# Attention output items later among the units, two expert loads sent earlier, four idle products ahead of the gather

## What is computed

```python
for l in range(DEPTH_2):                      # DEPTH_2 = 1
    h = rms_norm_2(x, norm_mix_w[l])
    p = h @ w_in[l]
    y_rw = rwkv7_mixer(p[..., :RW_COLS], ...)  # 8 heads of 64, a recurrence over tokens
    y_fox = fox_mixer(p[..., RW_COLS:], ...)   # 8 heads of attention with forget gates
    x = x + concatenate([y_rw, y_fox]) @ w_out[l]
    h = rms_norm_2(x, norm_ffn_w[l])
    x = x + hierarchical_moe(h, ...)           # 64 experts, 2 for each token
# rwkv7 step: S = S * w_t + (S a_t) b_t^T + v_t k_t^T ;  y_t = S r_t
# an expert:  (silu(x @ w_gate) * (x @ w_up)) @ w_down,  1024 x 512, 1024 x 512, 512 x 1024
```

## Time and profile before

| | |
|---|---|
| median of 3 runs | 1488.3 us (1487.18 to 1490.58) |
| the profiled execution's own time | 1499.18 us |
| its span in the profile | 1497.3 us |
| TensorE busy | 1129.1 us, 75% |
| VectorE, ScalarE, GpSimd busy | 342.0, 218.3, 68.2 us |
| read from HBM | 461.41 MB |
| granted TensorE clock, mean | 0.891 of full |

### The profile page before, as it was taken

One profiled execution on the slowest core, in us unless ns is written; L12 is line 12 of the kernel. 1 busy time (PEld: TensorE's weight loads), 2 busy tenths in 40 slices (PEclk: granted clock), 3 DMA queues, 4 the chain that ended last, 5 costly groups with the idle time before them and its releaser, 6 DMA issues.

```text
span 1497.3 us, 35673 instructions
## 1 busy us (share of the span) xinstructions
PE 1129.1 (75%) x15922; PEld 816.4 (55%) x15922; DVE 342.0 (23%) x993; ACT 218.3 (15%) x598; POOL 68.2 (5%) x119
## 2 busy tenths in 40 slices
PE   7999999999999887976565665666565666666565
PEld 4886578654885855754444444444444444444443
DVE  2544226520573144111111111111111111111111
ACT  1162106310152201110000000000000000000000
POOL 1100010000110110000000000000000000000000
PEclk9989999999999689998898889788888889888988
DMA  8733234215110069999999999999999999999997
GB/s 285 272 96 116 87 113 169 86 57 185 57 57 4 3 254 375 427 427 429 428 429 428 429 428 429 429 428 429 428 428 429 429 429 429 428 427 429 429 428 315
DMA packets 69029, 463.41 MB, mean 309 GB/s; under 512 B 14789, under 2 KB 18278, under 8 KB 44390
## 3 DMA queue, kind: packets, MB, share of 16 engines
q1 hardware_dynamic: 64784, 459.76, 74.5%
q10 hardware_dynamic: 4182, 2.72, 0.7%
HBM read 461.41 MB, written 1.05 MB: 309 GB/s over the span
## 4 chain that ended last, share of the span: by engine, by line
DMA 53%; PE 8%; DVE 1%; issue 1%; ACT 0%; SPq 0%; POOLq 0%; DVEq 0%; POOL 0%
DMA weight_slots<-in_exp_w_down_dram 53%; PE bank L2332 4%; PE bank L2323 1%; PE bank L2315 1%; PE bank L2297 0%; PE bank L2349 0%; ACT work_region L2253 0%; SPq L2167 0%; DVE normed_features L2454 0%; PE bank L2303 0%; DVE tokens L2532 0%; POOLq L2207 0%; DVE normed_features L2431 0%; DVE tokens L2514 0%; DVE tokens L2517 0%
## 5 line engine op out<-in xcount | busy, mean ns | idle before, releaser
L2323 PE MATMUL bank<-weight_slots,work_region 128*32 128x128 f32 x5120 | 182.2, 303 | 123.0 <-DMA weight_slots<-in_exp_w_up_dram 100.6
L2323 PEld LDWEIGHTS bank<-weight_slots,work_region 128*32 128x32 f32 x5120 | 157.0, 122 | 150.0 <-DMA weight_slots<-in_exp_w_up_dram 110.7
L2332 PE MATMUL bank<-weight_slots,work_region 128*32 128x256 f32 x1376 | 115.7, 489 | 90.8 <-DMA weight_slots<-in_exp_w_down_dram 88.1
L2323 PE MATMUL bank<-work_region 128*32 128x128 f32 x2560 | 92.7, 306 | 61.7 <-DMA work_region<-in_exp_w_up_dram 52.4
L2332 PEld LDWEIGHTS bank<-weight_slots,work_region 128*32 128x32 f32 x1376 | 58.7, 134 | 134.4 <-issue 98.2
L2323 PEld LDWEIGHTS bank<-work_region 128*32 128x32 f32 x2560 | 79.5, 123 | 75.3 <-DMA work_region<-in_exp_w_up_dram 57.5
L2253 ACT COPY work_region<-bank 128x256 f32<-128x256 f32 x64 | 23.8, 372 | 603.6 <-PE bank L2332 603.6
L2489 DVE TENSOR_SCALAR work_region<-work_region 128x128 f32<-128x128 f32 x128 | 38.5, 343 | 285.3 <-PE bank L2340 285.3
L534 PE MATMUL bank<-weight_slots,normed_features 128*128 128x512 f32 (+2 forms) x288 | 101.1, 508 | 2.1 <-DVE normed_features L792 2.1
L2332 PE MATMUL bank<-work_region 128*32 128x256 f32 x672 | 55.8, 484 | 45.5 <-DMA work_region<-in_exp_w_down_dram 44.8
L2500 DVE TENSOR_TENSOR work_region<-work_region,bank 128x128 f32<-128x128 f32 x64 | 23.9, 373 | 281.9 <-PE bank L2323 281.9
(11 more groups left out here) (431 smaller groups left out, 1253.2 us busy)
## 6 DMA issues: line engine op xcount, KB each, us to landing
weight_slots<-in_exp_w_up_dram SPq DMA_DIRECT2D x43, 2048.0 KB, 41.0
weight_slots<-in_exp_w_down_dram SPq DMA_DIRECT2D x43, 2048.0 KB, 40.7
weight_slots<-in_exp_w_gate_dram SPq DMA_DIRECT2D x43, 2048.0 KB, 41.7
work_region<-in_exp_w_gate_dram SPq DMA_DIRECT2D x21, 2048.0 KB, 41.8
work_region<-in_exp_w_up_dram SPq DMA_DIRECT2D x21, 2048.0 KB, 40.9
work_region<-in_exp_w_down_dram SPq DMA_DIRECT2D x21, 2048.0 KB, 40.7
weight_slots<-in_w_in_dram SPq DMA_DIRECT2D x16, 2048.0 KB, 9.9
weight_slots<-in_w_out_dram SPq DMA_DIRECT2D x6, 2048.0 KB, 8.5
```

The costliest lines, as they stand in the source:

```text
L2323: mm = nc.tensor.matmul(B[bank][BLK * j:BLK * (j + 1), 0:P], x[:, c], w[u][:, c, j * P:(j + 1) * P], start=c == 0, stop=c == KC - 1, tile_ ...
L2332: mm = nc.tensor.matmul(B[7][BLK * j:BLK * (j + 1), 0:256], hidt[u][:, BLK * k:BLK * (k + 1)], w_down[u][:, k, j * 256:(j + 1) * 256], sta ...
```

## The change

Three things. (a) In ORDER, and alike in TensorE's and ScalarE's programs, FO0 goes behind P21, FO1 behind TK1, FO2 behind MV1, FO3 behind F51. (b) The units' buffers are laid out slot by slot, so that slot 4 holds nothing that is read after item WV1 and slot 1 nothing that is read after the chunks' products; SyncE sends down 0 into slot 4 after WV1 and up 0 into slot 1 after chunk_made 4. The other two of EARLY stay where they were. (c) TensorE makes four products of 128 by 512 into a bank that is overwritten next, between the ranks and the gather.

```diff
@@ -1077,28 +1077,25 @@
-    room45 = carve(slot[:, 4:6].rearrange("p s n -> p (s n)"))
-    qt, kt = room45(4, T), room45(4, T)
-    pt = room45(4, 4, P)
-    sqk = room45(MT * 2 * NH, HD)
+    room4, room5 = carve(slot[:, 4]), carve(slot[:, 5])
+    qt, kt = room4(4, T), room4(4, T)
+    sqk = room4(MT * 2 * NH, HD)
+    pt = room5(4, 4, P)
-    room45 = carve(slot[:, 4:6].rearrange("p s n -> p (s n)"))
-    am, wu = room45(MT, NH, P), room45(MT, 2, NH, HD)
-    rbt, rkt = room45(MT, NH, CHUNK), room45(MT, NH, CHUNK)
-    reads = room45(2, CT, T)
-    a_, rx = reads[:, 0], reads[:, 1]
-    inverse_t, spare = room45(MT, NH, CHUNK), room45(MT, NH, CHUNK)
-    room01 = carve(slot[:, 0:2].rearrange("p s n -> p (s n)"))
-    btok, ktok, vtok = room01(MT, RW), room01(MT, RW), room01(MT, RW)
-    wt = room01(MT, CT, P)
-    kx = room01(CT, T)
-    state = room01(NCH, CT, HD)
-    ei = room01(CT, T)
+    room4, room5 = carve(slot[:, 4]), carve(slot[:, 5])
+    am, wu = room4(MT, NH, P), room5(MT, 2, NH, HD)
+    a_, rx = room4(CT, T), room5(CT, T)
+    reads = slot[:, 4:6, MT * NH * P:MT * NH * P + CT * T].rearrange("p x (i t) -> p x i t", i=CT)
+    inverse_t, spare = room4(MT, NH, CHUNK), room4(MT, NH, CHUNK)
+    rbt, rkt = room5(MT, NH, CHUNK), room5(MT, NH, CHUNK)
+    room0, room1 = carve(slot[:, 0]), carve(slot[:, 1])
+    vtok, wt, state = room0(MT, RW), room0(MT, CT, P), room0(NCH, CT, HD)
+    btok, ktok, kx, ei = room1(MT, RW), room1(MT, RW), room1(CT, T), room1(CT, T)
-    room_state = carve(state.rearrange("p q i d -> p (q i d)")[:, KC * LORA_W - D:])
-    f8 = room_state(MT, P)
-    kk_inv, ct = room_state(T), room_state(T)
+    room_tiles = carve(slot[:, 5, SLOT - 2 * MT * NH * CHUNK:])
+    f8 = room_tiles(MT, P)
+    kk_inv, ct = room_tiles(T), room_tiles(T)
@@ -1132,8 +1129,8 @@
-    ORDER = """TA0 TA1 AR0 AR1 FO0 KR0 KR1 TV0 TV1 FO1 P20 P21 FO2 P40 P41 FO3 P80 P81 TK0 TK1 G40 G41 MV0 MV1 Q0 Q1 TB0 TB1 F50 F51
-        BONUS WU0 WV0 WU1 WV1 WT0 WT1""".split()
+    ORDER = """TA0 TA1 AR0 AR1 KR0 KR1 TV0 TV1 P20 P21 FO0 P40 P41 P80 P81 TK0 TK1 FO1 G40 G41 MV0 MV1 FO2 Q0 Q1 TB0 TB1 F50 F51
+        FO3 BONUS WU0 WV0 WU1 WV1 WT0 WT1""".split()
@@ -1169,9 +1166,13 @@
                 sp.wait_ge(S["rkv_done"], 2 * (h + 1))
                 dst = slot[:, WO2_S[h], :].rearrange("p (k n) -> p k n", k=KC)
                 sp.dma_start(dst, wout[0, :, h * 512:(h + 1) * 512].rearrange("(k p) n -> p k n", p=P)).then_inc(loaded[WO2_S[h]], 16)
+            sp.wait_ge(S["item_made"], ORDER.index("WV1") + 1)
+            load_first_experts(sp, a, mem, EARLY[0:1])
+            sp.wait_ge(S["chunk_made"], 4)
+            load_first_experts(sp, a, mem, EARLY[1:2])
             sp.wait_ge(S["bonus_ready"], MT)
             sp.wait_ge(S["y_made"], MT)
-            load_first_experts(sp, a, mem, EARLY)
+            load_first_experts(sp, a, mem, EARLY[2:])
             for i in range(2):
                 sp.wait_ge(S["out_done"], 3 + i)
                 load_first_experts(sp, a, mem, LATE[i:i + 1])
@@ -1342,26 +1343,26 @@
 
             take(am[:, 0, :, 0:HD], "TA0", NH, HD)
             take(am[:, 1, :, 0:HD], "TA1", NH, HD)
-            fox_out(0)
             whole(vtok[:, 0], "TV0")
             whole(vtok[:, 1], "TV1")
+            for m in range(MT):
+                take(P2[:, m], f"P2{m}", NH, CHUNK)
+            fox_out(0)
+            for m in range(MT):
+                nc.scalar.copy(P4[:, m], view(bank(f"P4{m}")[:, :], NH, 2, CHUNK)[:, :, 0]).then_inc(S["power_copied"], 1)
+            for m in range(MT):
+                nc.scalar.copy(P8[:, m], view(bank(f"P8{m}")[:, :], NH, 2, CHUNK)[:, :, 1]).then_inc(S["power_copied"], 1)
+            for m in range(MT):
+                whole(ktok[:, m], f"TK{m}")
             fox_out(1)
             for m in range(MT):
-                take(P2[:, m], f"P2{m}", NH, CHUNK)
+                take(am[:, m, :, HD:P], f"MV{m}", NH, HD)
             fox_out(2)
             for m in range(MT):
-                nc.scalar.copy(P4[:, m], view(bank(f"P4{m}")[:, :], NH, 2, CHUNK)[:, :, 0]).then_inc(S["power_copied"], 1)
+                take(Q[:, m], f"Q{m}", NH, CHUNK)
+            for m in range(MT):
+                whole(btok[:, m], f"TB{m}")
             fox_out(3)
-            for m in range(MT):
-                nc.scalar.copy(P8[:, m], view(bank(f"P8{m}")[:, :], NH, 2, CHUNK)[:, :, 1]).then_inc(S["power_copied"], 1)
-            for m in range(MT):
-                whole(ktok[:, m], f"TK{m}")
-            for m in range(MT):
-                take(am[:, m, :, HD:P], f"MV{m}", NH, HD)
-            for m in range(MT):
-                take(Q[:, m], f"Q{m}", NH, CHUNK)
-            for m in range(MT):
-                whole(btok[:, m], f"TB{m}")
             src = bank("BONUS")
             nc.scalar.copy(bonus.rearrange("p m h -> p (m h)"), src[:, 0:MT * NH]).then_inc(S["act_took"], 1)
             for m in range(MT):
@@ -1616,21 +1617,18 @@
             turn("TA1", a_, 1)
             pe.wait_ge(S["scaled"], 5)
             of_features("AR", aa)
-            fox_out(0)
             of_features("KR", kx)
             pe.wait_ge(S["shifted"], 14)
             turn("TV0", v_, 0)
             turn("TV1", v_, 1)
-            fox_out(1)
             for m in range(MT):
                 pe.wait_ge(S["n_turned"], m + 1)
                 of_blocks(f"P2{m}", NT[:, m], N[:, m])
-            fox_out(2)
+            fox_out(0)
             for m in range(MT):
                 pe.wait_ge(S["power_turned"], m + 1)
                 pe.wait_ge(S["g_ready"], 1)
                 of_two(f"P4{m}", P2T, m, slice(0, 2))
-            fox_out(3)
             for m in range(MT):
                 pe.wait_ge(S["power_turned"], MT + m + 1)
                 needs(f"P4{m}")
@@ -1638,6 +1636,7 @@
             pe.wait_ge(S["ends_ready"], 1)
             turn("TK0", ei, 0)
             turn("TK1", ei, 1)
+            fox_out(1)
             for m in range(MT):
                 pe.wait_ge(S["power_turned"], 2 * MT + m + 1)
                 needs(f"P8{m}")
@@ -1645,6 +1644,7 @@
             for m in range(MT):
                 needs("KR0", "KR1", f"TV{m}")
                 of_blocks(f"MV{m}", AKT[:, m], view(vtok[:, m], NH, HD), HD)
+            fox_out(2)
             for m in range(MT):
                 pe.wait_ge(S["no_turned"], m + 1)
                 pe.wait_ge(S["f_turned"], m + 1)
@@ -1655,6 +1655,7 @@
             for m in range(MT):
                 needs(f"Q{m}")
                 of_blocks(f"F5{m}", G[:, m], Q[:, m])
+            fox_out(3)
             pe.wait_ge(S["rk_ready"], CT)
             out = bank("BONUS")
             for m in range(MT):
@@ -2064,6 +2065,7 @@
 NBUF = 3
 FIRST = 4
 NSORT = 2 * T
+WARM = 4
 
 
 def expert_slots(mem):
@@ -2083,7 +2085,7 @@
         sp.dma_start(buffers[name][e], src).then_inc(mem[name + "_in"][e], 16)
 
 
-EARLY = [("up", 0), ("down", 0), ("gate", 1), ("gate", 0)]
+EARLY = [("down", 0), ("up", 0), ("gate", 0), ("gate", 1)]
 LATE = [("up", 1), ("down", 1), ("gate", 2), ("up", 2), ("down", 2)]
 
 
@@ -2289,6 +2291,9 @@
             nc.tensor.matmul(B[5][:, 2 * NE:3 * NE], const("ones"), member[:, 0], start=True, stop=False)
             nc.tensor.matmul(B[5][:, 2 * NE:3 * NE], const("ones"), member[:, 1], start=False, stop=True).then_inc(S["ranked"], 1)
 
+            for _ in range(WARM):
+                nc.tensor.matmul(B[6][:, :], ident, XN[:, 0:512], start=True, stop=True)
+
             def first_rows_of():
                 pe.wait_ge(S["first_ready"], 1)
                 for h in range(2):
```

## The result

The changed kernel took **1494.86 us** (median of 20 runs, 1486.92 to 1499.69) against 1489.22 us for the kernel before (20 runs on the same chip, 1483.34 to 1495.21): **ratio 1.0037, 95% interval 1.0023 to 1.0051**, so 5.6 us slower. 1488.7 us and no measurable difference had been forecast.

The account below looks back on a forecast made before the run. The stream of expert weight loads was taken to bound the end, its restart waiting for gate_done(0). Order -1.0, loads +3.5 and idle products -2.1 summed to +0.4 on 1488.3: 1488.7 us, eight-in-ten range 1481 to 1494.

Parts of the forecast that it names:

- (a): FO items moved among the units: reordering +0.2 us, half clock 3.6 against 4.8; sum -1.0 us, bounds -4.7 and +2.0.
- (b): Two early loads: no gain, regrouping 0, instruction packets delayed +1.4 to +2.1 us per load; sum +3.5, bounds 0 and +4.2.
- (c): Idle products before the gather: gather 3.6 us instead of 6.13, VectorE's copy earlier, -2.1 us; bounds -2.5 and +2.5.
- the moment of the restart: At gate_done(0), the first expert's gate product: the hole before it takes all the early loads' gain, 0 us.
- rival 1: Instruction loading hidden in the units' new order, no stops, full clock: 1474 us; chance 0.12 shared with a loads-gain rival.
- Rival 3: Early stops among the units also lower the clock, +2.0 us for the order, total +3.4: 1491.7 us; chance 0.27.
- The wider hole ahead of the restart: Sign for the loads: DMA queue drains near 581.4 instead of about 583.9, ahead of the line 2160 issue.

Follow-up runs that it names:

- e1: Only the FO items' new order, against the kernel before: 1490.62 us, ratio 1.0006.
- e3: Only the four idle products before the gather, against the kernel before: 1489.62 us, ratio 1.0005.
- e4: New order and idle products, without early loads or regrouped buffers, against the kernel before: 1485.78 us, ratio 0.9976.
- e7: The kernel before, unchanged, run again as a yardstick: 1486.79 us, ratio 0.9989.
- e9: Only the regrouped buffers, nothing sent early among the units, against the kernel before: ratio 0.9991.
- e12: New order and idle products without the early loads, a repeat of e4, against the kernel before: 1490.13 us, ratio 0.9988.
- e14: Four idle products as in e3, plus three shorter ones in TensorE's waits behind the gather, against the kernel before: ratio 0.9989.
- e2: Only the regrouped buffers and two early loads, old order, no idle products, against the kernel before: 1496.08 us, ratio 1.0042.
- e5: New order and two early loads, without idle products, against the kernel before: 1494.74 us, ratio 1.0039.
- e6: Two early loads and idle products, items in the old order, against the kernel before: 1492.99 us, ratio 1.0031.
- e8: The changed kernel, all three parts, run again as a yardstick against the kernel before: 1493.83 us, ratio 1.0031.
- e13: As e2, but only half of each of the two matrices sent early, against the kernel before: ratio 1.0014.
- e10: As e2, but only down 0 sent early, after WV1, against the kernel before: ratio 1.0012.
- e11: As e2, but only up 0 sent early, after chunk_made 4, against the kernel before: ratio 1.0012.

## Why the prediction was wrong

**Where the time went, over all profiles.** Because single executions scatter, the stages are compared as means: of the eight profiles without early loads (before, e1, e3, e4, e7, e9, e12, e14) and the five with both whole loads (e2, e5, e6, e8, after). The stage is from WT's last product to the first transposition of y, line 1775 in the kernel after. Its windows for e7 and for the kernel after:

```profile
494.11:521.97 27.86, 24.26 (x929) 22.02 (x929) 12.02 (x28) 2.90 (x8) 2.49 (x4) 0.82 0.02 4
```

```profile
497.98:532.09 34.11, 27.35 (x928) 25.01 (x928) 12.11 (x28) 2.90 (x8) 2.49 (x4) 0.70 0.32 120
```

The same 928 products, the same work on the other engines. What differs is TensorE's idle time (3.6 against 6.8 us) and its busy time (24.26 against 27.35 us, at clock 0.82 against 0.70). Over the groups:

| mean of | stage | TensorE busy | idle | clock |
|---|---|---|---|---|
| 8 without early loads | 28.5 us | 24.8 | 3.7 | 0.80 |
| 1 with half loads (e13) | 30.8 us | 25.4 | 5.4 | 0.78 |
| 5 with both loads | 34.0 us | 26.9 | 7.1 | 0.74 |

The stage is 5.5 us longer. The single loads stand between (e10 32.5, e11 30.1). The products between the stops are the same in every run, so the stage can be cut at them (means in us):

| part of the stage | 8 without | 5 with both loads | difference |
|---|---|---|---|
| WT's end to the resume at the chunks' products | 4.5 | 6.9 | +2.4, all in the stop (0.9 to 3.3) |
| the next 128 products, without a stop | 7.1 | 8.3 | +1.2, lower clock |
| from there to the resume at the write products | 7.3 | 9.8 | +2.5, all in the stop (0.2 to 2.7) |
| the rest, with two more stops | 9.7 | 9.1 | -0.6: stops 2.7 to 1.2, lower clock +0.9 |

**The failing step is the term of the two loads, (b), +3.5 us.** Its mechanism held: the moment of the restart took the loads' gain whole, the regrouping shows no cost, and the packets behind the loads came late, at the two places named. Its size failed in two ways.

The waits were priced at +1.4 to +2.1 us for each load, after a stop in the steady stream of loads, with +4.2 as the upper bound. The two stops behind the loads grew by 2.4 and 2.5, +4.9 together. TensorE's whole idle time in the stage grew by only 3.4, near the 3.5 of the forecast, but that is luck: the two later stops, which the prediction didn't look at, shrank by 1.5.

The clock behind such a wait was put at nothing; the prediction priced half clock for the stops in the units alone, under (a). The seven profiles with a stop of 1.89 us or more at the chunks' products needed 8.2 to 8.3 us for the 128 products behind it, granted clock 0.50 or 0.51. The nine with a stop of 1.1 or less needed 5.9 to 8.3, clock 0.50 to 0.77. The clock falls among these products in every profile; after the long stop it is down from the start. Behind the write products it was 0.50 to 0.68 in five of the six profiles with the whole of up 0 in flight, and 1.00 in the other ten. There it cost next to nothing (+0.1 in the 128 products and the stop behind them): where these products ran slowly, the stop of 0.8 to 1.4 us behind them was gone. e10 and e11 put each of the two drops behind its own load. Whether the stop lowers the clock or the load in flight does is not separated; that e13's second half load, with a stop of 0.38, left the clock at 1.00 speaks for the stop.

In the timed runs the loads cost +5.7 us, and their uncertainty of some 2 us would still allow 4.2. That the upper bound was too low is shown by the traces, not by the times.

The Trainium skill ("DMA: Bandwidth & Descriptors", Queues, rings and completion order) lets a DMA engine drain a whole packet, typically 9 to 17 descriptors, from one queue before it switches to another. The prediction took one 16 KB piece of a load in the trace for such a packet and so came to 1.2 us for both loads; that price is refuted, since the two stops grew by 4.9. The rule itself is neither borne out nor refuted here, because no row tells how many pieces make one of its packets. A load of 128 pieces on 16 engines is 8 for each (an estimate); if a piece is a descriptor, an engine's whole share would go ahead of the instructions, which is near what the traces have. When the awaited packet began to move, 97 to 118 of the 128 pieces of down 0 had begun in the six profiles with it, and 124 to 128 of up 0 in its six.

**(a), the order.** The stops came where they were derived, in other sizes: KR 1.6 to 2.2 (2.0 forecast), P2 0.9 to 1.5 (1.6), P8 0.4 to 0.7 (1.0), MV 1.9 to 2.2 (1.3), FO3 0.2 to 0.9 (1.9, in F5). That crossing a block's boundary is "mostly hidden" (the Trainium skill, "Runtime: NRT & Kernel Launch", Instruction fetch mechanics) does not hold in this order either, and rival 1 is out. The stretch from TA0 to WT's end was forecast from one execution, which took 55.2 us. That was the dearest of all: the nine other profiles of the old order took 49.5 to 52.7, mean of the ten 51.0; the six of the new order took 50.7 to 52.0, mean 51.3. So the -1.0 was really +0.3 in the profiles, and -0.6 us in the timed pairs; neither is told from nothing. The half clock that the reordering was to relieve, 4.8 us, is a trait of that execution, not of the kernel.

**(c), the idle products.** The gather went from 5.2 to 6.1 us to 3.67 in every profile with them, and VectorE's copy came right behind its earlier work. But in four of the six profiles with them alone as in the change, the first expert's gate products, 3.70 us in all nine profiles without them, took 5.34 to 5.37. TensorE in e3:

```profile
566.75 3.67 PE L2301 MATMUL bank<-normed_tokens,normed_features 128*128 128x512 f32 x8 [0.29 <-issue]
...
573.44 5.37 PE L2327 MATMUL bank<-weight_slots,tokens 128*32 128x128 f32 x128 [0.78 <-DVE tokens L2521]
```

From the gather's start to the restart of the stream it is 10.4 us without and 9.7 us with idle products, on the mean: -0.7 us, not -2.1. The two executions that kept the clock have 8.7. In most executions the stretch of half clock is not removed but comes 7 us later, still ahead of gate_done(0). Whether filling the waits in between would keep it away stays open (e14).

**The sum.** By the stages: +0.3, +5.5 and -0.7, and the stage behind (y's transposes to the output projection's products) 0.8 shorter with the loads, which is not told from its scatter (18.0 to 21.2 us): +4.3 us; measured +5.6, interval 3.4 to 7.6. Against the forecast of +0.4 the loads made 2.0 of the difference, the idle products 1.4 and the order 1.3, less that 0.8. The measured 1494.86 lies just above the forecast range of 1481 to 1494. Rival 3, the one for slower, had the right sign by another cause: it placed the lost clock in the units.

**What else the profile was to show.** The wider hole ahead of the restart did not come: the queue ran dry near 574.3, 1.4 us ahead of the issue, against 2.7 before. The last three loads are sent when the experts begin (557.0). The first data of a load moves 1.0 us behind its issue, the dense part some 2.3 us behind it (499.0 behind 496.66), and three times 4.9 us from there is 574.0, whatever went out earlier. The gap that the two loads leave opens further ahead, between the gate loads and 546.81. It costs nothing either way.

**Versions that might beat both.** Order and idle products without the loads gave 0.9976 and, again, 0.9988, the second interval holding 1. No version of this study is surely faster than the kernel before.

## What to carry to other kernels

A large load sent into a stretch in which DMA is idle isn't free if an engine there uses up its instructions faster than they are loaded. Look first for "issue" stops and instruction packets in the stretch. Then price the wait from a row with a load like it, add the clock that the products behind it may lose, and follow the next stops too, since they can shrink. If nothing waits for the load, leave it where it was. Where the clock varies, one profiled execution is a sample: take terms of one to three microseconds from several, or expect them to be gone in the next; and when a half-clock stretch is chased away, look for it in the next products on the way to the same moment.

## What the runs showed of the hardware

A 16 KB packet of instructions that was wanted while a 2048 KB load was in flight moved when 97 to 128 of the load's 128 pieces had begun, in all twelve such cases, although the load was spread over the DMA engines. Counted from WT's end it came at 1.7 to 2.3 us without a load, at 3.2 with 1024 KB and at 4.2 to 5.1 with 2048 KB. Behind a TensorE stop of 1.9 us or more the next 128 products ran at a mean granted clock of 0.50 to 0.51, in seven profiles of seven; behind stops of up to 1.1 us at 0.50 to 0.77. A stop of 0.8 to 1.4 us for instructions was gone where the 128 products ahead of it ran at a mean clock of 0.68 or less, in five profiles, and there in the eleven where they ran at 1.00. Idle products of the full width kept the granted clock at 1.00 through the gather in all seven profiles with them, and in four of the seven the gate products that begin 7 us behind the gather's start fell to half clock, which they did in none of the nine without.
